# Layer norms by chunk of tokens, beside the matmuls around them

## The reference

```
x = layer_norm(a*x + mamba2_mixer(x))           # norm 0; in and out projections around a scan
x = layer_norm(a*x + square(relu(x@w_up))@w_down)   # norm 1; D 1024, hidden 4096
x = layer_norm(a*x + diff_attention(x, k, v))   # norm 2; 8 heads, k and v from x
x = layer_norm(a*x + square(relu(x@w_up))@w_down)   # norm 3
layer_norm(x) = (x - mean(x)) * rsqrt(var(x) + eps) * g + b     # over the 1024 features
```

## Time and profile before

| | |
|---|---|
| median of three runs | 3373.28 us (3372.2 to 3375.8) |
| profiled execution | 3373.14 us, span 3371.3 us |
| busy, TensorE | 3227.9 us (96%) |
| busy, VectorE / ScalarE / GpSimd | 1978.9 (59%) / 1000.0 (30%) / 869.2 us (26%) |
| mean granted clock of TensorE | 0.967 of full speed |

### The profile page before, as it was taken

How to read it: one execution, slowest core, us unless ns; L and a number is a source line. 1 busy time by engine, 2 the same in 40 slices (tenths; PEclk the granted TensorE clock), 3 DMA queues, 4 the chain that set the end, 5 groups by cost and what they waited for, 6 DMA issues and landing times.

```text
span 3371.3 us, 51878 instructions
## 1 busy us (share of the span) xinstructions
PE 3227.9 (96%) x20874; PEld 3091.5 (92%) x20874; DVE 1978.9 (59%) x2897; ACT 1000.0 (30%) x2433; POOL 869.2 (26%) x394
## 2 busy tenths in 40 slices
PE   7999999999996999999999899999987999999997
PEld 7899999999996999999998888888866999999996
DVE  6677777777777733443445767666667634333336
ACT  4544444444441311111110343443433211111112
POOL 2111111111111343333333222222201433343331
PEclk9999999999997999999999899999987999999997
DMA  3111111111110114311111322222210111111111
GB/s 115 54 45 54 59 55 56 47 61 56 43 62 15 38 45 150 132 63 44 45 50 38 97 76 82 76 76 82 80 47 13 51 44 47 48 45 51 44 51 51
DMA packets 86370, 201.11 MB, mean 60 GB/s; under 512 B 9416, under 2 KB 47176, under 8 KB 85616
## 3 DMA queue, kind: packets, MB, share of 16 engines
q1 hardware_dynamic: 35552, 139.54, 12.1%
q10 hardware_dynamic: 50592, 58.37, 5.6%
HBM read 166.86 MB, written 39.60 MB: 61 GB/s over the span
## 4 chain that ended last, share of the span: by engine, by line
issue 64%; PE 21%; POOLq 6%; POOL 6%; SPq 1%; DVE 1%; ACT 0%; DMA 0%; DVEq 0%; ACTq 0%
PE jb L364 21%; POOL wl L323 6%; POOLq L333 6%; SPq L302 1%; PE aux L546 0%; DVEq L1313 0%; ACT acc L1063 0%; DMA wraw<-in_wstream 0%; DVE acc L1314 0%; DVE acc L1560 0%; DMA acc<-in_xT 0%; POOLq L347 0%; POOLq L330 0%; DVE lnq L1564 0%; DVE xl L1312 0%
## 5 line engine op out<-in xcount | busy, mean ns | idle before, releaser
L364 PE MATMUL jb<-xh,wh 128*128 128x344 f32 x2616 | 843.1, 322 | 7.2 <-POOL wl L323 3.7
L364 PE MATMUL jb<-xl,wh 128*128 128x344 f32 x2616 | 837.2, 320 | 0.0
L364 PE MATMUL jb<-xh,wl 128*128 128x344 f32 x2616 | 837.0, 320 | 0.0
L323 POOL TENSOR_TENSOR wl<-wraw,wh 128x1024 fp32r<-128x1024 f32 x225 | 550.1, 2445 | 845.7 <-ACT wh L882 822.4
L331 POOL TENSOR_TENSOR wh<-wraw,one 128x1024 fp32r<-128x1024 f32 x164 | 318.8, 1944 | 1591.3 <-PE jb L364 887.1
L1344 DVE TENSOR_TENSOR acc<-jb,acc 128x344 f32<-128x344 f32 x504 | 254.4, 515 | 449.1 <-PE jb L364 445.5
L364 PEld LDWEIGHTS jb<-xh,wh 128*128 128x128 f32 x2616 | 493.0, 188 | 8.9 <-POOL wl L323 4.5
L364 PEld LDWEIGHTS jb<-xh,wl 128*128 128x128 f32 x2616 | 492.9, 188 | 0.0
L364 PEld LDWEIGHTS jb<-xl,wh 128*128 128x128 f32 x2616 | 492.8, 188 | 0.2
L364 PE MATMUL jb<-hh,wh 128*128 128x344 f32 x1536 | 492.2, 320 | 0.0
L364 PE MATMUL jb<-hl,wh 128*128 128x344 f32 x1536 | 490.9, 320 | 0.0
(11 more groups left out here) (271 smaller groups left out, 5049.3 us busy)
## 6 DMA issues: line engine op xcount, KB each, us to landing
wraw<-in_wstream SPq DMA_DIRECT2D x225, 512.0 KB, 3.2
pre<-in_state ACTq DMA_DIRECT2D x16, 512.0 KB, 4.3
out_ssm_s<-pre ACTq DMA_DIRECT2D x16, 512.0 KB, 3.5
kgat<-in_cache_k SPq DMA_DIRECT2D x16, 512.0 KB, 5.3
vgat<-in_cache_v SPq DMA_DIRECT2D x16, 512.0 KB, 6.5
past<-kgat ACTq DMA_DIRECT2D x8, 1024.0 KB, 5.8
past<-vgat ACTq DMA_DIRECT2D x8, 1024.0 KB, 5.7
acc<-in_xT SPq DMA_DIRECT2D x8, 516.0 KB, 6.7
```

The source lines that it names most:

```text
L323: nc.gpsimd.tensor_tensor(wl[slot][:], wraw[:, slot], wh[slot][:].bitcast(F32), ALU.subtract).then_inc(w_split, 1)
L364: last = mm(jb[:, c, 0:CW], w[slot][:, j * kt + k], x[:, k, cols], start=(k == 0 and p == 0), stop=(k == kt - 1 and p == 2))
```

## The change

The last output stages run over chunks outside and output tiles inside (`by_chunk`), for which the four weight units of a last down projection stay resident: two in the slots, one in an extra buffer, one in a part of the hidden block that is already used (`home`). The norm of chunk c is made while chunk c + 1 is multiplied: `norm_beside` puts its mean, variance and spread behind groups 0, 4 and 6 of the next chunk. Chunk 2 is normed beside three jobs of the next stage instead of two (the third unit is resident too): q, k and v of head 0, or three of the hidden block's four. VectorE and ScalarE get orders written out by hand, in which additions, pieces of the norm and evictions follow each other. `scale` no longer has g in it and takes four tiles at a time; `shift` applies g and b on ScalarE, into `xh` and again into `acc`; ALPHA moves into the first addition of the next sub-layer, and the pass at the norm's end goes. `low` and the semaphores `ln_norm`, `ln_hi` and `ln_lo` go by halves of a chunk. Squares of a chunk have one buffer, so those of chunk c + 1 wait for the variance of c. Head 0's evictions of q, k and v are all ahead of `queries_in(0)`. GpSimd's loops are written out. In the last head, whose output projection has one unit, `finish` runs by chunk as well. Norm 3 has no stage behind it: its chunk 2 comes last.

The diff, cut to its core (TensorE, then ScalarE from `shift`, then VectorE from `first`):

```diff
-UP_ORDER_AFTER_NORM = [(j, c) for c in range(NCH) for j in range(2)] + UP_ORDER[6:]
+AFTER_NORM = [(0, 0), (1, 0), (2, 0), (0, 1), (1, 1), (2, 1), (1, 2), (0, 2), (2, 2)]
+UP_ORDER_AFTER_NORM = AFTER_NORM + UP_ORDER[9:]
+LAST_DOWN = (U_ATT - 4, UNITS - 4)
+AFTER = (U_MLP0, U_ATT, U_MLP1)
...
+        def home(u):
+            for first in LAST_DOWN:
+                if first < u < first + 4:
+                    return (extra, slots[0], spare(0))[u - first - 1]
+            for l, first in enumerate(AFTER):
+                if u == first + 2:
+                    return (extra, spare(1), extra)[l]
+            return slots[u % 2]
...
+            def split(u):
+                pool.wait_ge(raw_in[u % 2], 16 * (u // 2) + 16)
+                begun = u
+                for first in LAST_DOWN:
+                    if first < u < first + 4:
+                        begun = (first, first + 1, first + 1)[u - first - 1]
+                for l, first in enumerate(AFTER):
+                    if first <= u < first + 3:
+                        begun = ((first, first + 1, first), (first - 2, first, first))[l % 2][u - first]
+                if u > 1:
                     pool.wait_ge(unit_begun, begun)
...
+            def norm_beside(l, c, k):
+                if c and k == 0:
+                    mean(l, c - 1)
+                if c and k == 4:
+                    variance(l, c - 1)
+                if c and k == 6:
+                    spread(l, c - 1)
+
+            def by_chunk(l, at, kt, rh, rlo):
+                per = 8 // kt
...
                 for c in range(NCH):
+                    for k in range(KD):
+                        x = c * KD + k
...
+                        pe.wait_ge(bank_free[x % 3], credits + x // 3)
...
                         last.then_inc(chunk_full, 1)
+                        norm_beside(l, c, k)
+
+            def jobs_after_norm(at, l):
...
+                for x, (j, c) in enumerate(AFTER_NORM):
...
+                    for k in range(KD):
+                        if k % 4 == 0:
+                            pe.wait_ge(s["ln_lo"], 6 * l + 2 * c + 1 + k // 4)
...
+                            if k == 0 and p == 0 and x in (0, 7, 8):
+                                last.then_inc(unit_begun, 1)
                     last.then_inc(chunk_full, 1)
+                    if x == 0:
+                        mean(l, 2)
+                    if x == 3:
+                        variance(l, 2)
+                    if x == 4:
+                        spread(l, 2)
...
+                by_chunk(2 * layer + 1, at, 4, hh[1], hl[1])
+
+            by_chunk(0, after_scan, 2, yh, yl)
             mlp(0)
-            layer_norm(1)
...
+                def shift(c, g):
+                    act.wait_ge(s["ln_norm"], 6 * l + 2 * c + g + 1)
+                    for k in range(4 * g, 4 * g + 4):
+                        if l < 3:
+                            af(xh[:, k, cols], acc[:, k, cols], ACT.Identity, scale=g_, bias=b_)
+                        last = af(acc[:, k, cols], acc[:, k, cols], ACT.Identity, scale=g_, bias=b_)
+                    last.then_inc(s["ln_hi"], 1)
...
+                squares(0, 0)
+                squares(0, 1)
                 root(0)
+                squares(1, 0)
+                squares(1, 1)
+                shift(0, 0)
+                shift(0, 1)
                 root(1)
...
+                shift(1, 0)
+                evict(0)
+                shift(1, 1)
+                evict(1)
+                squares(2, 0)
+                squares(2, 1)
+                evict(2)
+                evict(3)
                 root(2)
+                evict(4)
+                shift(2, 0)
+                shift(2, 1)
+                evict(5)
...
+            layer_norm(1, first_head)
+            for x in range(6, 9):
+                first_head(x)
             queries_in(0)
             keys_in(0)
...
-            for c in range(NCH):
-                take(c, done, rawv[:, c * CW:(c + 1) * CW], ACT.Copy)
             values_in(0)
...
+                if first:
+                    last = stt(acc[:, k, cols], acc[:, k, cols], ALPHA, jb[:, c, 0:CW], ALU.mult, ALU.add)
...
+                def scale(c, g):
+                    tt(v, v, aux[:, 2 * c, 0:CW].unsqueeze(1).to_broadcast([P, 4, CW]), ALU.mult).then_inc(s["ln_norm"], 1)
+                def low(c, g):
+                    tt(xl[v], acc[v], f(xh[v]), ALU.subtract).then_inc(s["ln_lo"], 1)
...
+                adds(0, 1, 2, 3, 4, 5, 6, 7)
+                adds(8)
                 drain()
+                centre(0, 0)
+                adds(9)
+                centre(0, 1)
+                adds(10, 11)
                 add_squares(0)
+                adds(12, 13)
                 invert_root(0)
+                adds(14, 15)
+                adds(16)
+                drain()
+                centre(1, 0)
+                adds(17)
+                centre(1, 1)
+                scale(0, 0)
+                adds(18)
+                scale(0, 1)
+                adds(19)
                 add_squares(1)
+                adds(20)
+                if l < 3:
+                    low(0, 0)
+                adds(21)
+                if l < 3:
+                    low(0, 1)
+                invert_root(1)
+                adds(22, 23)
                 drain()
...
+                scale(1, 0)
+                scale(1, 1)
+                centre(2, 0)
+                centre(2, 1)
+                low(1, 0)
+                up(0)
+                low(1, 1)
+                up(1)
                 add_squares(2)
+                up(2)
+                up(3)
                 invert_root(2)
+                up(4)
+                scale(2, 0)
+                scale(2, 1)
+                low(2, 0)
+                low(2, 1)
+                up(5)
```

More of the change, by code:

```diff
@@ L347, in _ @@
-            with pool.Fori(U_POOL // 2, (UNITS - 1) // 2) as i:
-                split(0, 16 * i + 16, 2 * i)
-                split(1, 16 * i + 16, 2 * i + 1)
-            split(0, 16 * ((UNITS - 1) // 2) + 16, UNITS - 1)
+            for u in range(UNITS):
+                if 3 <= u < U_POOL:
+                    pool.wait_ge(w_hi, u - 2)
+                    low(u)
+                else:
+                    split(u)
         @block.tensor
@@ new lines, in mean, with variance @@
+            def mean(l, c):
+                pe.wait_ge(s["ln_sum"], 3 * l + c + 1)
+                mm(ln_bank(c)[:, 0:CW], ones[:, 0:P], ln0[:, c * CW:(c + 1) * CW], start=True, stop=True).then_inc(s["ln_mu"], 1)
+            def variance(l, c):
+                pe.wait_ge(s["ln_add"], 3 * l + c + 1)
+                for b, (t0, _) in enumerate(blocks):
+                    for k in range(4):
+                        last = mm(ln_bank(c)[:, 500 + b:501 + b], squares_in[l][:, k, t0:t0 + P], ones[:, 0:1],
+                                  start=(k == 0), stop=(k == 3))
+                last.then_inc(s["ln_var"], 1)
@@ new lines, in spread @@
+            def spread(l, c):
+                pe.wait_ge(s["ln_inv"], 3 * l + c + 1)
+                for b, (t0, skip) in enumerate(blocks):
+                    last = mm(ln_bank(c)[:, t0 + skip:t0 + P], rstd[:, 1, 3 * c + b:3 * c + b + 1].to_broadcast([P, P]),
+                              ident[:, skip:P], start=True, stop=True)
+                last.then_inc(s["ln_scale"], 1)
+            def norm_beside(l, c, k):
[5 more added lines that the diff above has]
+                    spread(l, c - 1)
@@ L822, in _ @@
             finish(at, HEADS_B)
-            layer_norm(2)
             mlp(1)
-            layer_norm(3)
+            mean(3, 2)
+            variance(3, 2)
+            spread(3, 2)
         @block.scalar
@@ L1277, in _ @@
             af(lam[:, 0:2], lam[:, 0:2], ACT.Exp).then_inc(s["lam_exp"], 1)
-            _, done = at.job()
-            for c in range(NCH):
-                take(c, done, rawv[:, c * CW:(c + 1) * CW], ACT.Copy)
             values_in(0)
```

377 lines of the change are left out of this document (194 added, 183 removed).

## The result

The changed kernel takes 3416.56 us (median of four runs, 3414.96 to 3418.7) against 3373.47 (3372.2 to 3375.8) on the same chip: a ratio of 1.0127, 95% interval 1.0110 to 1.0145, 43 us slower. The prediction had the side (slower, 0.73) and 3393 us with a range to 3406: the time lies 10.6 us outside it. The profiled execution has a span of 3416.9 us.

The account below looks back on a forecast made before the run. TensorE, busy 96% of the span, was taken as the bound, not paying in four layer norms. Norms summed to 0.6 + 2.9 + 8.5 - 7.3 = +4.7 us, about +20 with clock falls: 3373.3 + 20 = 3393 us, range 3371 to 3406.

Parts of the forecast that it names:

- The chain before the first score: Start of attention: swaps, table load and rotations all come after v's last matmul, 16.9 us with nothing hiding them.
- The tail from the last projection: End of the kernel, norm 3: some 28 us behind the last projection, before 47.
- (c): Attention's start is not late, a chain step having waited for something fixed in time: takes back at most 13, 3380; chance 0.11.
- (d): Faster: waits within stages vanish because VectorE runs ahead by its three banks, some 85 us, 3290; chance 0.08.
- The walk: Steps three engines through each norm in listed order with traced durations; norm 0's waits 30.3 us, norm 2's 38.8.
- The step that failed: Clock falls at three, three, three and two waits in the norms, 4.5 us half speed behind each: about +20 us.
- the sum at full clock: All four norms without clock falls: 0.6 + 2.9 + 8.5 - 7.3 = +4.7 us.
- the slow start: Start of norm 0's stage, where TensorE begins at slow clock as before: 2.1 us.
- rival (b): Clock stays low through a norm, 9 to 12 us behind each wait: +39 to +51, 3412 to 3424; chance 0.10.
- the prediction's upper bound, 6.3: Slow clock of 6.3 us after each fall in the norms, as after 1913.4: +30 us.
- ScalarE's second write: Norms: ScalarE writes `acc` too, sixteen shifts a chunk instead of eight, 0.57 us each, 4.6 us for eight.
- the late start of attention: Norm 1: q, k and v end 4.5 us earlier, but the first score comes at 1921.9, net +8.5.

Follow-up runs that it names:

- dense: Changed kernel with each variance made by four full-width fp32 matmuls instead of twelve one-column ones, no spread, wide root and reciprocal: 3401.7 us, ratio 1.0076.
- filler: Changed kernel with 24 to 48 extra full-width matmuls into an unused bank ahead of four variances in norms 0, 1 and 3: 3407.7 us, ratio 1.0102.
- after_r2: Changed kernel with squares in fp32r and one-pass variances, 12 records instead of 24 for a chunk: 3393.6 us, ratio 1.0056.
- no_acc: Changed kernel with ScalarE writing only `xh`, not `acc`, in norms 0 to 2 (residual misses gain and shift): 3395.7 us, ratio 1.0064.
- behind02: Changed kernel with norms 0 and 2 behind their stages, chunk 2 still among the jobs, one buffer of squares: 3418.4 us, ratio 1.0125.
- The fillers: Changed kernel with extra full-width matmuls in all waits of over 3 us inside the norms: 3400.8 us, ratio 1.0085.
- best_after: Changed kernel with extra matmuls in all norms, fp32r variances, and q and k swaps before v's last eviction: 3374.1 us, ratio 1.0000.
- before_r2: Kernel before the change with squares in fp32r and one-pass variances: 3350.0 us, ratio 0.9924.

## Why the prediction fell short

**Right.** The side; the waits and their places; what replaces what. Longest waits, forecast and measured: `variance(1)` 8.4, 8.1 and 5.1 against 8.21, 7.94 and 5.03 (norms 0, 2, 1); `variance(0)` 4.3, 5.1 and 1.0 against 3.99, 4.94 and 0.83; chunk 2's first half 5.9 and 4.5 against 5.76 and 4.26. ScalarE's shifts come every 0.565 us (forecast 0.57). The chain before the first score is 16.74 us (16.9). The tail from the last projection (3387.4) to the end is 29.5 us (forecast some 28). Rivals (c) and (d) are out: neither was attention early nor did a wait vanish. The walk had the waits too high, in norm 0 by 4.8 us of 30.3 and in norm 2 by 8.8 of 38.8 (30.0 measured). Its 3378 at full clock was not measured: no run keeps the clock up throughout.

**The step that failed** is in the part on the clock: "I count a fall at each (three, three, three and two), and 4.5 us at half speed behind each, as at 1044.8". It was worth 15 to 17 us over the sum at full clock (4.7). The norms measure 47.0 us in all (13.8 + 16.2 + 15.3 + 1.8), which is 42 over it. Half of the half-speed work given above is 61 us lost; of this the waits that were forecast too long take back 4.8 in norm 0 and 8.8 in norm 2, and 2 were in the forecast as the slow start. Norm by norm this estimate gives 12, 11, 13 and 10 us over the sum at full clock, and 13.2, 7.7, 12.4 and 9.1 were measured. So the clock is nearly all of it. In norm 0 the step gives three stretches of 4.5 us, 13.5 in all; measured were four, with 34 us of work at half speed. Three things were wrong in it.

- The kind of matmul. The length was read where full-width matmuls follow the wait. Behind most waits of a norm twelve one-column matmuls stand first. They run at half speed and don't bring the clock up, so that the full-width work behind them pays its own time at half speed as well: 10.4 us in place of 4.5. dense shows it (full-width work in the same place: full speed right behind), and so did and the mean clock of 0.59 in the earlier trace rows, which the prediction used only for rival (b).
- The length itself. Behind the wait for chunk 2 (5.76 us) full-width matmuls alone follow, and the clock came up 8.7 us behind it, in filler, after_r2 and dense 8.4 to 9.5. Behind norm 1's wait of 4.26 us it came up after 2.8 us in one execution and after 9.6 in another, with the same matmuls behind. So one reading of 4.5 was no price; even the prediction's upper bound, 6.3, was under most of them. What sets the length stays open.
- The count missed the variances that hardly wait. There are five in the changed kernel, behind 0.67 to 1.26 us, and at each the clock falls in or behind the variance (1122.15, 1836.97). filler shows the fall behind a variance at full speed, no_acc behind one with no wait at all (at two of three places). With 12 records in place of 24 (after_r2) it falls at one of the five, with the full-width variance (dense) at none.

Rival (b), with 9 to 12 us behind each wait, had 3412 to 3424 and a chance of 0.10. Its time is the measured one, and norm 0's stretches of 6.8 to 10.2 us are near its price; its reason covers the variances but not the wait for chunk 2. Its "against: now projections lie between" overlooked the variance that stands first behind most waits. The Trainium skill ("TensorE: Matmul & The Clock Gate", section "HAM oscillation — how this bites in real kernels") has bursts between waits start cold each time. The trace agrees that the price is paid at each wait: in the changed kernel's norms the clock is at half speed behind every one of 3.6 us or more. The length of such a start was anything from 2.8 us (from 1912.66) to 14.9 (from 2607.10, with a wait of 1.95 us in it).

**What the same waits are made of.** ScalarE's second write was priced right for each instruction, but stood only inside the waits of the walk. As a term of its own it weighs 21 us, in norm 0 about half wait and half the clock behind the wait. Beside that the order, which the prediction spent most words on, is worth 3 to 4 us a norm in norms 0 and 2, and the place beside the stage next to nothing (behind02). For norm 3 the sum at full clock had -7.3 and +1.8 was measured: TensorE works 19.7 us at half speed there, nearly as long as before (20.5). The fillers make it -3.8, the fp32r variance -6.6 and both -8.2, but the same edits give the old order -7.4 and -7.5. Like with like, the new order gains next to nothing in norm 3.

**Norm 1** stays 9 to 12 us up with the fillers, the fp32r variance, the wide variance or no second write. That is near its sum at full clock (+8.5), which is the late start of attention; only best_after, with the early swaps besides, comes to +2.2.

**Open** is how norm 0's last 4 us without the second write divide between the third unit's splits and the rest.

## What to carry to other kernels

Splitting one long stall into several short ones saved no waiting here (norm 0: 25.5 us against 15.6), and the clock is paid anew at each (projections beyond their full-clock time: 14.5 us against 6.1). Price a wait by what is issued behind it, take the length at half speed from several places with the same kind of matmul behind them, and carry its spread as the range. Count the short one-column bursts too. Before a norm is moved, make its pieces cheap where they are: halving the variance's passes won 24 us with the order untouched, and the new order, with fillers, fp32r variance and early swaps, only came back to where it started. When work moves to another engine, run once without it: a term that looks hidden may stand ahead of the evictions.

## What was not expected of the hardware

- 24 one-column records, begun at full speed behind a wait of 0.67 to 1.26 us, had half speed in or behind them at all five places of the changed kernel, for 3.4 us or 6.8; 12 records (1.50 us) at one of five (after_r2), 8 full-width records (2.58 us) at none (dense). With no wait ahead 24 records did it at two of three places (no_acc).
- A reciprocal of 344 columns took 2.31 us where an addition of the same width takes 0.52.
- Behind the same line of matmuls half speed lasted 3.4 us, and began 1.5 us late, after a wait of 3.50 us, and 8.7 us after one of 5.76. Behind a wait of 4.26 us it lasted 2.8 us in one execution and 9.6 in another.
- In the four kernels with the fp32r variance norm 0's stage starts 5 to 7.5 us later (before_r2 at 1050.11, after_r2 at 1052.27, the kernel before at 1044.76), all of it added in the mixer, whose code is the same but for one small copy at the start and the place of the buffers. Why stays open. The lengths of the norms don't contain it, the times do.
